# Weight slots moved to one place modulo 512 bytes, and x laid out 1024 bytes a chunk for 256 tokens

## What is computed

```
h = concatenate([meta, x], axis=1)                      # 272 tokens
for layer in range(2):
    u = rmsnorm(h, mix_norm_pre[layer])
    u = hybrid_mixer(u, ...) if layer == 0 else retention_mixer(u, ret_w_in, ret_w_out)
    h = h + rmsnorm(u, mix_norm_post[layer])
    u = swiglu(rmsnorm(h, ffn_norm_pre[layer]), w_gate, w_up, w_down)   # D_FF = 5632
    h = h + rmsnorm(u, ffn_norm_post[layer])
return h[:, 16:]                                        # the meta tokens are dropped

def swiglu(h, w_gate, w_up, w_down):
    return (silu(h @ w_gate) * (h @ w_up)) @ w_down
def retention_mixer(h, w_in, w_out):
    q, k, v, gate = split(h @ w_in)                     # 8 heads: 2, 2, 4 and 4 tiles of 128
    o = rms(chunk_retention(rotate(q), rotate(k) / 16, v))
    return (silu(gate) * o) @ w_out
```

## The kernel before

| operand | before, modulo 512 | after, modulo 512 |
|---|---|---|
| w_hi slot 0 / slot 1 | 160 / 224 | 160 / 160 |
| w_lo slot 0 / slot 1 | 288 / 352 | 288 / 288 |
| x_hi and x_lo, 256 tokens, chunk k | 192 + 64 k (wraps round) | 352 for every k |
| x_hi and x_lo, 272 tokens, chunk k | 128 + 64 k | unchanged |
| mid_hi and mid_lo, 256 tokens | 352 for every k | unchanged |
| third_hi, third_lo | 448 | unchanged |

## Time and profile before

### The profile page before, as it was taken

How to read it: one execution, slowest core, us unless ns; L and a number is a source line. 1 busy time by engine, 2 the same in 40 slices (tenths; PEclk the granted TensorE clock), 3 DMA queues, 4 the chain that set the end, 5 groups by cost and what they waited for, 6 DMA issues and landing times.

```text
span 2930.1 us, 58319 instructions
## 1 busy us (share of the span) xinstructions
PE 2904.7 (99%) x22768; PEld 2832.0 (97%) x22768; DVE 1688.7 (58%) x2402; ACT 1365.5 (47%) x1994; POOL 183.9 (6%) x213
## 2 busy tenths in 40 slices
PE   9999999999999999999999999999999999999998
PEld 9889999999999999999999999999999998899987
DVE  4887665755544555546555555555466556555555
ACT  5556665644333343345444444444454443344443
POOL 0111100200000000001111111010010000000000
PEclk9999999999999999999999999999999999999999
DMA  5222324444445554554444444444544555545554
GB/s 211 101 96 87 122 98 143 162 151 179 172 165 174 180 179 177 178 177 166 147 162 168 165 165 172 158 180 178 188 156 173 185 186 202 191 182 186 185 200 159
DMA packets 74101, 483.87 MB, mean 165 GB/s; under 512 B 8909, under 2 KB 9337, under 8 KB 23456
## 3 DMA queue, kind: packets, MB, share of 16 engines
q1 hardware_dynamic: 73808, 482.30, 46.2%
q0 software_dynamic: 208, 0.39, 0.0%
HBM read 480.41 MB, written 2.10 MB: 165 GB/s over the span
## 4 chain that ended last, share of the span: by engine, by line
PE 92%; DVE 5%; ACT 1%; issue 1%; DMA 0%; POOL 0%; DVEq 0%; SPq 0%; ACTq 0%; POOLq 0%
PE ps L596 91%; DVE w_lo L2317 1%; DVE ps L2252 0%; DVE x_lo L2243 0%; DVE h L2258 0%; DVE w_lo L2175 0%; PE ps L984 0%; PE ps L1384 0%; DMA h<-in_x_t 0%; ACT x_hi L1540 0%; DVE bias L2448 0%; DVE kq L2360 0%; DVE conv_acc L2346 0%; ACT w_hi L1927 0%; ACT w_hi L1461 0%
## 5 line engine op out<-in xcount | busy, mean ns | idle before, releaser
L596 PE MATMUL ps<-x_hi,w_hi 128*128 128x272 f32 (+1 forms) x4944 | 1435.5, 291 | 4.9 <-ACT x_hi L1540 2.1
L596 PE MATMUL ps<-x_hi,w_lo 128*128 128x272 f32 (+1 forms) x4944 | 1411.2, 285 | 0.2 <-DVE u L2583 0.2
L596 PE MATMUL ps<-x_lo,w_hi 128*128 128x272 f32 (+1 forms) x4944 | 1407.2, 285 | 0.8 <-DVE x_lo L2243 0.4
L2175 DVE TENSOR_TENSOR w_lo<-raw,w_hi 128x1024 fp32r<-128x1024 f32 (+2 forms) x893 | 1010.7, 1167 | 384.5 <-ACT w_hi L1461 369.8
L1461 ACT ACTIVATE w_hi<-raw 128x1024 fp32r<-128x1024 f32 (+2 forms) x839 | 824.1, 1010 | 514.6 <-PE ps L596 452.1
L596 PEld LDWEIGHTS ps<-x_hi,w_hi 128*128 128x128 f32 x4944 | 933.5, 189 | 13.5 <-issue 6.3
L596 PEld LDWEIGHTS ps<-x_lo,w_hi 128*128 128x128 f32 x4944 | 933.2, 189 | 3.9 <-DVE x_lo L2243 2.3
L596 PEld LDWEIGHTS ps<-x_hi,w_lo 128*128 128x128 f32 x4944 | 930.2, 188 | 1.1 <-DVE u L2583 0.5
L596 PE MATMUL ps<-mid_hi,w_lo 128*128 128x272 f32 (+1 forms) x1216 | 346.3, 285 | 0.0
L596 PE MATMUL ps<-mid_hi,w_hi 128*128 128x272 f32 (+1 forms) x1216 | 346.2, 285 | 0.0
L596 PE MATMUL ps<-mid_lo,w_hi 128*128 128x272 f32 (+1 forms) x1216 | 345.2, 284 | 0.0
(11 more groups left out here) (357 smaller groups left out, 2532.6 us busy)
## 6 DMA issues: line engine op xcount, KB each, us to landing
raw<-in_w_up SPq DMA_DIRECT2D x172, 1024.0 KB, 4.8
raw<-in_w_ret_in SPq DMA_DIRECT2D x94, 1024.0 KB, 4.8
raw<-in_w_down SPq DMA_DIRECT2D x64, 704.0 KB, 4.0
raw<-in_w_rows SPq DMA_DIRECT2D x44, 1024.0 KB, 4.8
raw<-in_w_heads SPq DMA_DIRECT2D x32, 1024.0 KB, 4.8
raw<-in_w_ret_out SPq DMA_DIRECT2D x32, 1024.0 KB, 4.8
raw<-in_w_mix_early SPq DMA_DIRECT2D x16, 768.0 KB, 4.3
raw<-in_w_latent SPq DMA_DIRECT2D x8, 1024.0 KB, 4.8
```

The source lines that it names most:

```text
L596: return nc.tensor.matmul(o, lhs, rhs, start=start, stop=stop)
L2175: V.tensor_tensor(w_lo[:, slot, cut], raw[:, slot, cut], w_hi[:, slot, cut], ALU.subtract).then_inc(lo_ready, count)
```

## The change

The second slots of `w_hi` and `w_lo` move: each slot is now 8192 bytes long in place of 8256, and the 4 x 64 bytes that this frees stand between the two tensors (`w_between`, 128 bytes) and behind them (`w_rear`, 128 bytes more). For 256 tokens, x is stored and read through `x_of`, which packs the 16 chunks 1024 bytes apart from byte 224 of x on; for 272 tokens nothing changes. No instruction is added, removed or moved on any engine; the operands' addresses alone differ. All readers and writers of the 256-token x go through `x_of`.

```
@@ -185,7 +185,6 @@
             return ctx.enter_context(nc.semaphore(name))


-        SLOT = 16 * P + 16
         h = sb("h", [P, KC, T])
         x_hi = sb("x_hi", [P, KC, T], F32R)
         with ExitStack() as mixed:
@@ -195,9 +194,10 @@
         u = sb("u", [P, KC, T])
         raw = sb("raw", [P, 2, 16 * P])
         sb("w_front", [P, 8])
-        w_hi = sb("w_hi", [P, 2, SLOT], F32R)
-        w_lo = sb("w_lo", [P, 2, SLOT], F32R)
-        sb("w_rear", [P, 8])
+        w_hi = sb("w_hi", [P, 2, 16 * P], F32R)
+        sb("w_between", [P, 32])
+        w_lo = sb("w_lo", [P, 2, 16 * P], F32R)
+        sb("w_rear", [P, 40])
         with ExitStack() as turned:

             h_rows = sb("h_rows", [P, 2, D], F32, turned)
@@ -287,6 +287,15 @@
             rot_a = sb("rot_a", [P, 2, T], F32, second)
             ret_sq = sb("ret_sq", [P, 4, SEQ], F32, second)
             ret_r = sb("ret_r", [P, SEQ], F32, second)
+
+        X_FRONT = 56
+
+        def x_of(x, t0):
+
+            if t0 == 0:
+                return x[:, :, 0:T]
+            return x[:, :, :].rearrange("p c t -> p (c t)")[:, X_FRONT:X_FRONT + KC * SEQ].rearrange(
+                "p (c t) -> p c t", c=KC)

         u_rows = flat[:, 0:2 * D].rearrange("p (b d) -> p b d", b=2)
         out_rows = u_part[:, :, :].rearrange("p c t -> p (c t)")[:, 0:2 * D].rearrange("p (b d) -> p b d", b=2)
...
@@ -664,13 +673,14 @@

                 o = ps[:, BK_0, t0:T]
                 pe.wait_ge(x_hi_ready, KC * (norm // 2) + k + 1)
-                mm(o, w_hi[:, 0, k * P:(k + 1) * P], x_hi[:, k, t0:T], k == 0, False)
-                mm(o, w_lo[:, 0, k * P:(k + 1) * P], x_hi[:, k, t0:T], False, False)
+                mm(o, w_hi[:, 0, k * P:(k + 1) * P], x_of(x_hi, t0)[:, k], k == 0, False)
+                mm(o, w_lo[:, 0, k * P:(k + 1) * P], x_of(x_hi, t0)[:, k], False, False)

             def fresh_lo(norm, k, t0):

                 pe.wait_ge(x_lo_ready, KC * (norm // 2) + k + 1)
-                return mm(ps[:, BK_0, t0:T], w_hi[:, 0, k * P:(k + 1) * P], x_lo[:, k, t0:T], False, k == KC - 1)
+                return mm(ps[:, BK_0, t0:T], w_hi[:, 0, k * P:(k + 1) * P], x_of(x_lo, t0)[:, k],
+                          False, k == KC - 1)

             def fresh_pair(base):

...
@@ -708,8 +718,8 @@
                     if 0 <= j < KC:
                         if j % 8 == 0:
                             pe.wait_ge(lo_ready, 2 * (base + 1) + 1 + j // 8)
-                        pair = multiply(ps[:, BK_1, t0:T], 1, j, 1, lambda _: x_hi[:, j, t0:T],
-                                        lambda _: x_lo[:, j, t0:T], j == 0, j == KC - 1)
+                        pair = multiply(ps[:, BK_1, t0:T], 1, j, 1, lambda _: x_of(x_hi, t0)[:, j],
+                                        lambda _: x_of(x_lo, t0)[:, j], j == 0, j == KC - 1)
                         if j == 7:
...
                 def xh(k):
-                    return x_hi[:, k, t0:T]
+                    return x_of(x_hi, t0)[:, k]

                 def xl(k):
-                    return x_lo[:, k, t0:T]
+                    return x_of(x_lo, t0)[:, k]

                 if norm is None:
                     for s in range(2):
...

                 def high(k):
-                    nc.scalar.activation(x_hi[:, k, t0:T], h[:, k, t0:T], ACT.Copy, scale=gains[:, norm, k:k + 1]
+                    nc.scalar.activation(x_of(x_hi, t0)[:, k], h[:, k, t0:T], ACT.Copy, scale=gains[:, norm, k:k + 1]
                                          ).then_inc(x_hi_ready, 1)

...
                 dve.wait_ge(x_hi_ready, KC * (norm // 2) + k + 1)
-                V.scalar_tensor_tensor(x_lo[:, ds1(k), t0:T], h[:, ds1(k), t0:T], gains[:, norm, ds1(k)],
-                                       x_hi[:, ds1(k), t0:T], ALU.mult, ALU.subtract).then_inc(x_lo_ready, 1)
+                V.scalar_tensor_tensor(x_of(x_lo, t0)[:, ds1(k)], h[:, ds1(k), t0:T], gains[:, norm, ds1(k)],
+                                       x_of(x_hi, t0)[:, ds1(k)], ALU.mult, ALU.subtract).then_inc(x_lo_ready, 1)
```

More of the change, by code:

```diff
@@ L720, in fresh_three @@
                         cut, o = slice(n * P, (n + 1) * P), ps[:, BK_2, t0:T]
-                        mm(o, third_hi[:, cut], x_hi[:, n, t0:T], n == 0, False)
-                        mm(o, third_hi[:, cut], x_lo[:, n, t0:T], False, False)
-                        last = mm(o, third_lo[:, cut], x_hi[:, n, t0:T], False, n == KC - 1)
+                        mm(o, third_hi[:, cut], x_of(x_hi, t0)[:, n], n == 0, False)
+                        mm(o, third_hi[:, cut], x_of(x_lo, t0)[:, n], False, False)
+                        last = mm(o, third_lo[:, cut], x_of(x_hi, t0)[:, n], False, n == KC - 1)
                     if k < KC:
```

## The result

The changed kernel takes 2909.68 us (median of 4, 2909.59 to 2910.01) against 2932.0 us of the kernel before: a ratio of 0.9925, 95% interval 0.9912 to 0.9937. It is faster by 22.3 us, 0.76%. The forecast was 2899.9 us with a range of 2895 to 2905, so it had the sign and the place of most of the gain, but promised 9.8 us more than came. Each median's own executions lie within 0.5 us.

What follows compares the result with a forecast made beforehand. PE, busy 99% of the span, was taken as the bound, its matmul rate set by operand addresses. Savings of 29.3 + 3.5 - 0.7 = 32.1 us from 2932.0 gave 2899.9 us, range 2895 to 2905.

Steps and rivals of the forecast that it cites:

- step 1: 256-token x tiles in ret_in, up2 and up3: 131 tiles save 0.224 us each, 29.3 us (27.9 to 30.8).
- step 5: ACT and DVE work at new addresses: costed at nothing, since up3 showed 1.8 us of cover against 0.22 us a tile.
- the best case: Upper bound of the whole saving, all terms at their most favourable: 37 us.
- The price a tile: 256-token x tiles after the change: 5.45 us each, the middle of 5.46 and 5.44, in place of 5.674.
- Step 2: ret_out's second halves fall from 5.67 to 5.45 us: 3.5 us saved, up to 0.3 more from first halves.
- Step 3: down2 and down3, where weights are the moving operands: 22 groups lose 0.03 us each, -0.7 us (-2 to +1).
- Step 4: 272-token tiles: x does not move and both slots cost the same, so 0, with +-1 us as bounds.
- No change: Rival: ret_out's halves differ for another reason than the address, so the change does nothing; 2932 us, 3 in 100.
- x does not reach the cheap rate: Rival: x_lo's different offset modulo 2048 keeps x tiles at 5.67 us, only ret_out gains; 2929 us, 5 in 100.
- Part of it: Rival: x_lo's third of matmuls, or one stage such as ret_in with its restarts, stays dear; 2910 us, 5 in 100.
- Slower: Rival: one fixed bad relation holds for all 6384 matmuls, up to 125 ns each; 2972 us, 2 in 100.
- The Trainium skill's rule: PE never waits on another engine at SBUF and has a second read port for weights, so placement saves zero: 2932.

Runs made afterwards that it cites:

- ret_packed: The changed kernel with ret_in's 256-token tiles also reading x through the packed form (other values, same shapes, order and waits): 2902.81 us.
- slots_only: The kernel before with the weight slots moved alone, x staying 1088 bytes a chunk: 2929.73 us, ratio 0.9991.
- x_at_288: The changed kernel with x for 256 tokens 64 bytes lower, at 288 modulo 512: 2929.67 us, ratio 0.9993.
- w_lo_moved: The changed kernel with w_lo alone moved up by 64 bytes, to 352, w_hi staying at 160: 2938.57 us.
- both_moved: The changed kernel with both weight slots and the 256-token x moved up by the same 64 bytes, mid staying: 2914.94 us (one run).

## Why the prediction was wrong, step by step

**The step that failed is the count of step 1**, the 6384 matmuls or 133 tiles, of them "46 in ret_in", to which the price was applied. The count of 256-column matmuls is right, but those of ret_in do not read the packed x. `ret_tile` takes its operands itself, as `x_hi[:, k, t0:T]`, and the diff leaves that line alone; it must, since in ret_in tiles 2 to 7 need the same x for 272 tokens, and `FROM[4]` is 0, so x is stored there 1088 bytes a chunk. The sentence "All readers and writers of the 256-token x go through `x_of`" in the section on the change is wrong for ret_in, and so is the table's row on x. The number of columns in a row of the trace does not say how far apart the chunks lie; the line that reads them does. 46 x 0.224 = 10.3 us of the sum had no basis. Without them it is 32.1 - 10.3 = 21.8 us, against 22.3 measured. ret_packed shows the same from the other side: made to read packed x, these tiles fall to the cheap rate, and the time to 2902.81 us. What is left to 2899.9 is the 3.5 us of waits that step 5 held to be hidden, less small terms. (Step 1's own bounds come to 28.0 and 30.7 us in place of 27.9 and 30.8, and the best case to 37.4 in place of 37; that moves the range by less than 0.5 us.)

**The price a tile was right.** 5.45 forecast, 5.44 measured, the lower of the two bounds: the three dearer matmuls at the head of a half came from the switch between two rates, and in ret_out and up3 only the first half or tile still shows them (5.48 and 5.46 us). In ret_packed, where the tiles at the end of ret_in run at the cheap rate already, ret_out's first half takes 5.44 too. up3 gave 10.3 us (9.9 forecast). up2 gave 9.0 us with its opening, for 9.2 from 41 tiles.

**Step 2** (ret_out, 3.5 us): 4.0 us, the 0.3 us of the first halves included, as bounded.

**Step 3** (down2 and down3, -0.7 us): -0.6 us, as if slot 1 took on slot 0's time.

**Step 4** (272-token tiles, 0 with 1 us either way): up1 264.01 and 264.02 us; ret_in 0.25 us and what lies before it 0.26 us longer. In ret_in the growth is in the 256-token tiles, most of it in tile 9, which reads slot 1: 8.84 in place of 8.82 us. slots_only has the same 619.25 us for ret_in, so it comes from the slots' new place.

**Step 5** (work off PE hidden): right for the changed kernel; its waits over ret_in are those of before. As a statement on what 0.22 us a tile would uncover it was wrong for ret_in, had the change reached it. I took the cover from up3 and carried it over to a stage where DVE has a head's output to finish, and there 0.5 us a head is uncovered.

**The rivals.** "No change" and "x does not reach the cheap rate" are refuted: the modulus is 256, so the different distance modulo 2048 between x_lo and mid_lo does not matter. "Part of it" named ret_in as the stage that might stay dear and its time would have been 2910, right in size, but by luck: the mechanism that it gave is the one that ret_packed refutes. "Slower" stayed away, though its idea, that one fixed bad relation holds for every matmul, is real: x_at_288 and w_lo_moved are such cases and cost as much as wandering x or a little more, with 2938.57 us for the latter, slower than before. The Trainium skill's rule (SBUF — State Buffer, "SBUF: two separate sides") would have given 2932. both_moved and x_at_288 contradict it where the addresses of PE's two operands meet: up3 takes 5.44 us a tile in the changed kernel and with both operands moved, and 5.68 with x alone 64 bytes lower. Against its other statement, that PE waits at SBUF on no other engine, nothing here speaks: the rates are the same with ACT and DVE busy or idle.

## What to carry to other kernels

Before multiplying a price by a count, check at each line that issues those instructions that the edit reaches it; equal shapes in the trace are not equal addresses. Where one stage shows two rates for the same matmul, compare the operands' byte addresses, moving minus stationary, and look for stages that can be given the cheap distance: here it is worth 4.1% of a matmul (113.3 ns for 118.2). And check cover in the stage that gets faster, not in a similar one.

## What the runs showed of the hardware

- A stream of fp32r matmuls with 128 stationary and 256 moving columns at the 2.4 GHz clock runs at 113.33 ns each (272 cycles of that clock) if the moving operand starts 192 bytes (modulo 256) above w_hi and 64 above w_lo at every matmul. At 160 / 32, 128 / 0 and 192 / 0, and with x wandering over 32, 96, 160 and 224, it took 117.8 to 118.3 ns (5.65 to 5.68 us a tile).
- The rate belongs to the stream, not to the single matmul: with one bad distance in three all three matmuls take 117.5 to 118.3 ns, and at 64 / 192 the same code runs at 113.3 ns in one stage and at 118.9 ns in the next, reproducibly.
- With 272 moving columns it is 125.0 ns, and 124.4 ns with a fixed distance. Sixteen columns more thus cost 11 to 12 ns over the cheap rate of 256 columns, and 6 to 7 ns over the dear one.
- Why the distance matters was not shown. A collision of PE's two read streams within an address period of 256 bytes would fit, and no run here looked inside. What a 272-token layout with chunks a multiple of 256 bytes apart would give ret_in's 256-token tiles (1280 bytes would need 6 KB more a partition) was not tried either.
